# The end of an RWKV branch in another order, with other PSUM bank turns, and the first transposes of a product moved ahead

## What is computed

```python
u = rmsnorm(h, mix_pre_norm)
z = u @ w_in                                  # z_attn | z_rwkv | z_gate
o_attn = dilated_attention_branch(z_attn)     # 3 groups of 4 heads, blocks of 128 queries, softmax over all groups
o_rwkv = rwkv7_time_mix(z_rwkv, ...)          # 8 heads of 64, a recurrence over tokens, group norm, gate
gate_attn, gate_rwkv = split(sigmoid(z_gate))
merged = gate_attn * (o_attn @ w_attn_up) + gate_rwkv * (o_rwkv @ w_rwkv_up)
h = h + rmsnorm(merged @ w_out, mix_post_norm)
```

## Time and profile before

| | us |
|---|---|
| median of 3 runs | 926.79 |
| lowest, highest | 926.22, 926.84 |
| the profiled execution, its time | 926.23 |
| its span in the trace | 924.4 |
| PE busy in it | 903.4 (98%) |
| DVE, ACT, POOL busy | 598.1, 447.6, 44.4 |

### The profile page before, as it was taken

One profiled execution on the slowest core, in us unless ns is written; L12 is line 12 of the kernel. 1 busy time (PEld: TensorE's weight loads), 2 busy tenths in 40 slices (PEclk: granted clock), 3 DMA queues, 4 the chain that ended last, 5 costly groups with the idle time before them and its releaser, 6 DMA issues.

```text
span 924.4 us, 15532 instructions
## 1 busy us (share of the span) xinstructions
PE 903.4 (98%) x6632; PEld 761.9 (82%) x6632; DVE 598.1 (65%) x956; ACT 447.6 (48%) x724; POOL 44.4 (5%) x61
## 2 busy tenths in 40 slices
PE   7999999998999999999999999999999999999997
PEld 4999988777789988888889978776778798888885
DVE  4568977556855566656764577876863456666673
ACT  4775444436433444546443356483522445555571
POOL 0010000010000000000000440000000000000000
PEclk9999999999999999999999999999999999999999
DMA  9535333223667655555339674352626566665531
GB/s 336 183 122 153 95 99 101 80 92 95 225 249 238 218 182 183 185 202 203 115 115 212 144 225 151 111 182 92 226 92 205 138 182 182 183 185 187 204 108 45
DMA packets 131204, 150.78 MB, mean 163 GB/s; under 512 B 11808, under 2 KB 102176, under 8 KB 131008
## 3 DMA queue, kind: packets, MB, share of 16 engines
q1 hardware_dynamic: 129920, 145.57, 50.9%
q10 hardware_dynamic: 1216, 4.23, 1.2%
HBM read 148.73 MB, written 1.05 MB: 162 GB/s over the span
## 4 chain that ended last, share of the span: by engine, by line
PE 87%; DVE 7%; ACT 2%; issue 2%; DMA 1%; POOL 0%; POOLq 0%; ACTq 0%; DVEq 0%
PE psum L828 11%; PE psum L717 9%; PE psum L718 9%; PE psum L719 9%; PE psum L829 6%; PE psum L780 6%; PE psum L800 4%; PE psum L801 3%; PE psum L809 3%; PE psum L723 3%; PE psum L876 3%; PE psum L877 2%; PE psum L886 2%; PE psum L831 2%; PE psum L1683 1%
## 5 line engine op out<-in xcount | busy, mean ns | idle before, releaser
L1786 ACT ACTIVATE parts<-low 128x1024 fp32r<-128x1024 f32 (+3 forms) x246 | 248.3, 1044 | 81.5 <-PE psum L719 57.3
L2643 DVE TENSOR_TENSOR parts<-low,parts 128x1024 fp32r<-128x1024 f32 (+3 forms) x150 | 180.3, 1229 | 30.1 <-ACT parts L1786 29.9
L717 PE MATMUL psum<-parts 128*128 128x512 f32 (+2 forms) x424 | 170.3, 402 | 1.0 <-DVE parts L2643 1.0
L718 PE MATMUL psum<-parts 128*128 128x512 f32 (+2 forms) x424 | 164.0, 387 | 0.0
L719 PE MATMUL psum<-parts 128*128 128x512 f32 (+2 forms) x424 | 164.0, 387 | 0.0
L828 PE MATMUL psum<-parts 128*128 128x512 f32 x434 | 155.7, 398 | 0.0
L829 PE MATMUL psum<-parts 128*128 128x256 f32 x496 | 129.1, 281 | 0.0
L1786 ACT ACTIVATE high<-psum 128x512 f32<-128x512 f32 (+5 forms) x93 | 51.3, 563 | 150.6 <-PE psum L831 72.7
L829 PEld LDWEIGHTS psum<-parts 128*128 128x128 f32 x496 | 93.6, 189 | 5.7
L717 PEld LDWEIGHTS psum<-parts 128*128 128x128 f32 x424 | 80.0, 189 | 21.3 <-issue 3.1
L828 PEld LDWEIGHTS psum<-parts 128*128 128x128 f32 x434 | 81.7, 188 | 17.0
(11 more groups left out here) (322 smaller groups left out, 1355.3 us busy)
## 6 DMA issues: line engine op xcount, KB each, us to landing
low<-in_w_in_dram SPq DMA_DIRECT2D x40, 1024.0 KB, 5.2
low<-in_w_ffn_in_dram SPq DMA_DIRECT2D x44, 512.0 KB, 5.2
low<-in_w_ff_in_dram SPq DMA_DIRECT2D x16, 1024.0 KB, 5.6
low<-in_w_ff_out_dram SPq DMA_DIRECT2D x16, 1024.0 KB, 4.9
low<-in_w_ffn_out_dram SPq DMA_DIRECT2D x11, 1024.0 KB, 4.9
low<-in_w_out_dram SPq DMA_DIRECT2D x8, 1024.0 KB, 5.2
low<-in_w_ple_gate_dram SPq DMA_DIRECT2D x4, 1024.0 KB, 5.0
low<-consts_dram ACTq DMA_DIRECT2D x1, 2142.0 KB, 9.2
```

Of the source, the lines that this page charges most:

```text
L717: mm(o, l[0], r[0], start, False)
L718: mm(o, l[0], r[1], False, False)
L1786: return e.activation(o, a, ACT.Copy)
L2643: tt(rslot3(n, nk, width)[:, r, 0:w], slot3(n, nk, width)[:, r, 0:w], st.hi3(j)[:, r, 0:w].bitcast(F32), ALU.subtract) \
```

## The change

Seen from PE:

- `order_1` has another sequence of letters for the last part; `attention` begins one turn later (a second `yield` ahead of its rounds) and ends with six empty turns for seven.
- In `state(1)` three banks are skipped after the rhs step (`apart_from_scores`), so that u uses bank 5 for bank 6 and y bank 6 for 7; the transposes of `normed(0)` use bank 7 for bank 4, those of `normed(1)` bank 4 for 5, and the four `w_rwkv_up` products banks 5, 6, 7, 4 for 6, 7, 4, 5.
- The eight transposes of `turn_parts("wo1", 0)` stand between the third and the fourth `w_rwkv_up` product, where they stood behind the fourth.
- On ACT both columns of the first slot of `w_rwkv_up` are cut inside `up_a`, by the side of the `w_attn_up` products, and not at the end of `attention`; on DVE the first of them moves in the same way.

The number and the forms of the instructions are the same on every engine.

```diff
--- before.py
+++ after.py
@@ -549,7 +549,8 @@
               "wo2": (A["w_out_2"][0], [P + 26152, P + 28200, P + 19968, P + 17920], m2Hi, m2Lo)}
 
         def order_1():
-            return itertools.chain("msmsm" * 12, "msmsmms", "mms" * 10, "ms" * 4, "mms" * 7, "ms", "mms" * 6, "m" * 14, itertools.cycle("ms"))
+            return itertools.chain("msmsm" * 12, "msmsmms", "mms" * 10, "ms" * 5, "mmmmmms", "ms", "mms" * 2, "ms", "mms", "ms",
+                                   "mms" * 2, "ms" * 3, "mms", "m" * 6, itertools.cycle("ms"))
@@ -1226,6 +1227,11 @@
                     free[b] = [rw_act.at("x21", 1)]
                     yield
 
+                def apart_from_scores(i):
+                    if i == 1:
+                        for _ in range(3):
+                            next(rw_bank)
+
                 def state(i):
                     b = next(rw_bank)
                     o = bank(b)
@@ -1244,6 +1250,7 @@
                     t.then_inc(rw_pe.up("rhs", i), 1)
                     free[b] = [rw_dve.at("rhs", i)]
                     yield
+                    apart_from_scores(i)
                     b = next(rw_bank)
                     o = bank(b)
                     q.wait_ge(*rw_pool.at("ua", i))
@@ -1297,9 +1304,14 @@
                 yield from state(0)
                 yield from turns.paired(second(), normed(0))
                 yield from normed(1)
-                yield from up3("r", 4, rw_bank)
+                for n, _ in enumerate(up3("r", 4, rw_bank)):
+                    if n == 2:
+                        for _ in turn_parts("wo1", 0, mt, up_dve.at("m", 0, 1)):
+                            pass
+                    yield
 
             def attention():
+                yield
                 yield
                 for i in range(2):
                     for hh in range(2):
@@ -1360,7 +1372,7 @@
                         t.then_inc(at_pe.up("o", i, hh), 1)
                         free[b] = [at_act.at("o", i, hh)]
                         yield
-                for _ in range(7):
+                for _ in range(6):
                     yield
 
             def up3(tag, K, ring):
@@ -1395,7 +1407,7 @@
 
 
             turns.alone(ups)
-            turns.alone(turn_parts("wo1", 0, mt, up_dve.at("m", 0, 1)))
+            turns.alone(itertools.repeat(None, 2))
             first_rows = block("wo1", 0, (0, 2))
             for _ in range(3):
                 turns.go("wo", first_rows)
@@ -2102,7 +2114,8 @@
                 def state(i):
                     next(rw_bank)
                     yield
-                    next(rw_bank)
+                    for _ in range(4 if i == 1 else 1):
+                        next(rw_bank)
                     yield
                     y_banks.append(bank(next(rw_bank)))
                     if i == 0:
...
@@ -2161,9 +2175,7 @@
                 yield
                 up_rows("r", 0, 1, over, rw_dve.at("o", 0))
                 yield
-                for k in range(2):
-                    up_columns("r", k, over)
-                    yield
+                yield
 
             def up_columns(tag, k, over):
@@ -2184,7 +2196,8 @@
             def up_a():
                 for n in range(4):
                     if n < 2:
-                        up_columns("r", 2 + n, at_pe.at("o", 1, 1))
+                        for k in range(2):
+                            up_columns("r", 2 * n + k, at_pe.at("o", 1, 1))
                     yield
 
             ups = up_a()
@@ -3047,8 +3064,6 @@
                 yield
                 up_rows("r", 0, 1)
                 yield
-                up_columns("r", 0)
-                yield
 
             def up_columns(tag, k):
@@ -3064,6 +3079,8 @@
             def up_a():
                 reads = up("a", [main_act.at("g1", 1, 1)], read_a)
                 for n in range(4):
+                    if n == 0:
+                        up_columns("r", 0)
                     if n < 3:
                         up_columns("r", 1 + n)
                     next(reads)
```

## The result

| | before | changed |
|---|---|---|
| median of 6 runs each, us | 926.46 | 930.40 |
| lowest, highest, us | 926.05, 926.84 | 928.71, 932.05 |
| the profiled execution, us | 926.23 | 932.05 |
| its span, us | 924.4 | 929.8 |

The ratio is 1.0047 (95% interval 1.0037 to 1.0057): the change makes the kernel slower, by 4.3 us after the ratio and by 3.9 us between the medians. The six runs of the changed kernel come in two groups, 928.71 to 929.51 with a mean granted clock of TensorE of 0.998 or 0.999, and 931.29 to 932.05 with 0.995.

What follows compares the result with a forecast made beforehand. PE, busy 98% of the span, was taken as the bound, so order moves only its waits: -5.45 + 5.9 + 2.6 - 0.1 = +3.0 us, 929.2 for the profiled execution and 929.8 for the median, range 927.0 to 933.2.

Steps and rivals of the forecast that it cites:

- c: normed(0)'s transposes move from bank 4 to bank 7 and no longer wait for DVE's last score read: -2.35 us.
- d: The lowered clock behind the wait ahead of normed(0)'s transposes goes with that wait: -1.7 us.
- e: `received` stands right behind round 2's scores and waits for DVE's read of shared bank 4: +0.7 us.
- f: keyed(1, 0) takes y's bank 5 and waits for ACT's copy, queued behind round 2's two exps: +0.7 us.
- g: Round 2's transposes wait for DVE's scaling, behind reads of keyed(1, 0), group norm steps and a cut: +1.75 us.
- h: keyed(1, 1) stands right behind round 3's scores and waits for the reading of bank 4: +1.6 us.
- i: Round 4's transposes wait for the scaling behind a cut: +1.05 us, and 0.1 for the second pair's bank.
- third, fourth `w_attn_up` product start at: Starts 4.8 and 7.9 us after the first product, DVE's reads being late; +2.6 us in all, bounds 1.2 to 3.0.
- transposes for `w_out`, with the bank turns: Moved transposes lose 1.7 us of waits, mostly paid back inside the w_out product: net -0.1, between 0 and -1.7.
- rival A: Clock drops at new waits in rounds or up products, 1.7 us each: 931.5 with one, 933.2 with two; chance 0.25.
- The forecast with the clock kept: Whole kernel: waits as summed, no clock drop, 929.8 us (929.0 to 930.9); chance 0.44.
- Rival D: Whole kernel: bank 4 handoffs count, queues behind them are covered, the clock's gain is whole: 925.1 us; chance 0.04.

Runs made afterwards that it cites:

- e1: The kernel before with the bank turns alone (three banks skipped in state(1)), order, transposes and cuts as before; ratio 0.9973, median 923.1 us.
- e6: The changed kernel without the bank turns and with the transposes for w_out behind the last product; ratio 1.0071 to the kernel before.
- e2: e1 with the eight transposes for w_out also moved ahead of the last w_rwkv_up product; ratio 0.9985 to the kernel before, +1.1 us against e1.
- e13: The changed kernel itself, run again on another group's chip; ratio 1.0045 to the kernel before.
- e10: The changed kernel with ACT's copy of y(0) ahead of round 2's exps and one DVE cut ahead of reading the scores; ratio 1.0028 to the kernel before.
- e7: The changed kernel with DVE reading the first and second w_attn_up products ahead of the w_rwkv_up cuts; ratio 1.0016 to the kernel before.
- e5: The kernel before with only ACT's cuts of w_rwkv_up's first slot moved behind the last gate piece's read; ratio 1.0014, +1.3 us.
- e4: The changed kernel with the eight transposes for w_out back behind the last w_rwkv_up product; ratio 1.0037 to the kernel before.
- e9: The changed kernel with keyed(1, 1) in banks 6 and 7 in place of 4 and 7; ratio 1.0047 to the kernel before.
- e8: e1 with ACT's gate-slot cuts, DVE's round 3 cut and DVE's w_attn_up reads placed earlier; ratio 0.9941 to the kernel before, median 919.93 us.
- e12: The changed kernel joining e4, e7 and e10, with DVE's cut also behind round 4's scaling; ratio 0.9987 to the kernel before.

## Why the prediction was right

Forecast 929.8, measured 930.4, slower as forecast, to which the prediction gave a chance of 0.69. By its steps:

| step | forecast, us | measured, us |
|---|---|---|
| a, b: waits of rounds 1 and 3 | -0.8, -0.6 | gone |
| c: bank 4 ahead of `normed(0)` | -2.35 | gone; the turns do it (e1, e6) |
| d: its clock | -1.7 | -1.6, in some executions |
| e, f | +0.7, +0.7 | 0.65, 0.66 |
| g | +1.75 | 1.62 |
| h | +1.6 | 1.55 |
| i | +1.15 | 0.87 |
| third, fourth `w_attn_up` product start at | 4.8, 7.9 | 4.79, 7.85 |
| transposes for `w_out`, with the bank turns | -0.1 | -0.2 (e2), +1.15 (e13, 24.32 us) |
| a drop of the clock (rival A) | 1.7 each | 2.4, in 9 of 27 |

**The waits.** Every new wait stands in the place and with the releaser that the prediction named, and the terms e to i are off by less than 0.3 us. In the `w_attn_up` products the starts fit to 0.05; the second wait there is 1.29 (1.40 with the clock kept) for 1.7. The 0.5 to 0.6 at the last slot of `w_out` is missing in the first profile, and it is 1.20 in that of e13. The experiments take causes away: f and half of g (e10), the `w_attn_up` products (e7, e5), c (e1, e6). Terms e and i were not taken away on their own. Added up as the prediction writes them, the pieces of term i give 1.2 for its 1.15, and the fourth product's start comes to 8.0 for its 7.9; neither matters.

**The forecast with the clock kept** gave 929.8; the three runs with a mean clock of 0.998 or more took 928.7 to 929.5. Rival A with one drop gave 931.5; the other three took 931.3 to 932.05. So the forecast and rival A both came true, in different executions, and the median lies between them. The prediction took them for alternatives of the kernel; they are alternatives of a run. How near the median came to 929.8 is therefore in part luck: it depends on how many runs of a handful have the drop, and the four of e13, with none, have a median of 929.3. The better test of the sum leaves the clock out: without term d it gives +4.7, and the spans with the clock kept on both sides are 4.5 apart.

**Two steps were off.** The drop was priced by the earlier trace rows, 4 us at 0.57 of full, of which about 3.4 us are at the lower level. In the new place it lasts about 6.8 us (241.9 to 248.7), with 1.3 us of idle time inside, and costs 2.4. The prediction also thought of the waits of the products together (3.7 of 5.2 us idle); in the two traces with this drop the clock had fallen before the second of them. And the step on the transposes for `w_out` put all 1.7 us of the earlier trace rows to their new place. Its sum holds (e2's stretch is 22.99 us, before 23.17: -0.2), but 0.87 of it was the bank turns' work, which moved the last product out of bank 5, and the move itself costs 0.7 and with a late last slot up to 1.2 more. With that slot late, e13's +1.15 is outside the bounds of 0 to -1.7 that the step gave itself. The prediction walked through the new banks for `normed(0)` and the scores and not for this product; the expectations of e2 and e4 inherited that and missed by 1 us.

**On h** the prediction called the wait a handoff of bank 4. e9 shows it to be that only for a quarter (a third, by the starts): without the shared bank, 1.20 of the 1.55 us stand one product further on.

**Rival D**, the rule on shared banks taken alone, would have given 925.1. Its gain side was there (c, d), but the queues behind the handoffs were not covered.

## What to carry to other kernels

Where PE is busy 98% of the span, follow PE through the new order and set each handoff against the rows that stand ahead of the releaser in its own queue; the list of those gave the new waits to about 0.3 us here. A wait behind a shared bank is two things, the bank and the reader's queue: change the bank and look where the reader stands next, or move the reader ahead of the cuts and copies that nobody waits for yet, which here was worth some 3 us at a time (e7, e8) with no work removed. When banks are turned, go through every later tenant of every bank in the ring, since a turn made for one wait can give or take another much later: here 0.87 us, some 40 us behind the wait that it was made for.

## What the runs showed of the hardware

- The granted clock of TensorE can fall to 1.2 GHz behind the same waits in one execution and stay at 2.4 GHz in the next. After a single wait of 2.35 us it fell in the profile of before, 0.5 us behind the wait's end, and not in those of e5 and e6. Behind a wait of 1.91 us it fell in the profiles of the changed kernel and e4, 1.2 to 1.4 us behind the wait's end and ahead of the next wait, and not in those of e9, e10 and e13; by the mean clock it fell in 9 of 27 executions. The profiles of e1, e2, e7, e8 and e12, whose waits are 1.55 us or less, don't have it, and no mean under 0.998 stands in their 44 executions. A drop cost 1.6 us in the first place and 2.4 in the second. What decides between two executions is open.
- Under the lower clock, 512-column matmuls started 0.43 us apart, under the full one 0.23.
- The same 1 MB slot took 5.0 us from issue to landing in one execution and 6.3 in another, and this alone made a wait of 1.20 us.
